# A two-block transformer kernel: last stage with row tiles stationary, inversion products in exchanged partition halves, boundaries started by one tile

## The reference

```
# first block, 272 rows: h = [meta; x]
h = h + rms_norm(diff_attention(rms_norm(h)), post0)
h = h + rms_norm(pool_mixer(rms_norm(h)), post1)
# second block, 256 rows
u   = rms_norm(h, pre_mix)
z   = u @ w_in                                  # splits into rwkv7, MLA and gates
mix = (g_rw * (rwkv7(z) @ w_b1) + g_mla * (mla(z) @ w_b2)) @ w_out
h   = h + rms_norm(mix, post_mix)
up  = causal_dwconv(rms_norm(h, pre_ffn) @ w_up)
h   = h + rms_norm((gelu(gate) * val) @ w_down, post_ffn)
e   = p @ w_ple                                 # p: 256 x 256
h   = h + rms_norm(sigmoid(h @ w_ple_gate) * e, ple_norm)
```

## Time and profile before

| | us |
|---|---|
| median of 3 executions | 2595.68 |
| lowest, highest | 2595.41, 2595.91 |
| profiled execution | 2592.1 |
| its span, first to last instruction | 2590.1 |
| mean granted TensorE clock | 0.993 of full speed |
| TensorE busy | 2508.2 |
| VectorE busy | 1634.2 |
| ScalarE busy | 1186.3 |
| GpSimd busy | 133.1 |
| bytes read from HBM | 418.14 MB at 163 GB/s over the span |

### The profile page before, as it was taken

How to read it: one execution, slowest core, us unless ns; L and a number is a source line. 1 busy time by engine, 2 the same in 40 slices (tenths; PEclk the granted TensorE clock), 3 DMA queues, 4 the chain that set the end, 5 groups by cost and what they waited for, 6 DMA issues and landing times.

```text
span 2590.1 us, 52387 instructions
## 1 busy us (share of the span) xinstructions
PE 2508.2 (97%) x22570; PEld 2458.2 (95%) x22570; DVE 1634.2 (63%) x1904; ACT 1186.3 (46%) x1630; POOL 133.1 (5%) x75
## 2 busy tenths in 40 slices
PE   8999999999999999999998999989999999999997
PEld 7999999989999889889897999989999999999997
DVE  6666676656555688487465545476666666666675
ACT  5444555544434562352345434455444444444563
POOL 0000000003500021031000000000000000000000
PEclk9999999999999999999999999999999999999999
DMA  6444444344555453242242465545545555555543
GB/s 226 158 151 162 144 149 161 130 147 164 180 193 180 158 210 116 77 169 87 97 162 98 169 225 181 194 151 181 193 178 188 185 180 192 178 187 185 180 178 114
DMA packets 60346, 424.58 MB, mean 164 GB/s; under 512 B 6544, under 2 KB 8720, under 8 KB 9648
## 3 DMA queue, kind: packets, MB, share of 16 engines
q1 hardware_dynamic: 60000, 421.72, 45.5%
q0 software_dynamic: 208, 0.77, 0.1%
HBM read 418.14 MB, written 4.33 MB: 163 GB/s over the span
## 4 chain that ended last, share of the span: by engine, by line
PE 87%; DVE 8%; ACT 2%; issue 1%; POOL 1%; DMA 0%; DVEq 0%; SPq 0%; POOLq 0%; ACTq 0%
PE banks L225 26%; PE banks L227 25%; PE banks L226 25%; DVE weights_lo_sb L200 2%; PE banks L279 1%; PE banks L281 1%; PE banks L280 1%; PE banks L1259 1%; PE banks L1272 1%; PE banks L607 1%; PE banks L1271 1%; PE banks L623 1%; POOL sums_sb L1021 0%; PE banks L1313 0%; PE banks L1703 0%
## 5 line engine op out<-in xcount | busy, mean ns | idle before, releaser
L225 PE MATMUL banks<-xa_hi_sb,weights_hi_sb 128*128 128x256 f32 (+1 forms) x4608 | 1315.9, 286 | 42.4 <-DVE xa_lo_sb L398 19.0
L227 PE MATMUL banks<-xa_hi_sb,weights_lo_sb 128*128 128x256 f32 (+1 forms) x4608 | 1302.6, 283 | 0.0
L226 PE MATMUL banks<-xa_lo_sb,weights_hi_sb 128*128 128x256 f32 (+1 forms) x4608 | 1300.6, 282 | 0.0
L200 DVE TENSOR_TENSOR weights_lo_sb<-raw_weights_sb,weights_hi_sb 128x1024 fp32r<-128x1024 f32 x786 | 939.9, 1240 | 271.2 <-ACT weights_hi_sb L186 265.3
L186 ACT CAST weights_hi_sb<-raw_weights_sb 128x1024 fp32r<-128x1024 f32 x786 | 780.1, 1049 | 573.1 <-DMA raw_weights_sb<-weights 572.8
L225 PEld LDWEIGHTS banks<-xa_hi_sb,weights_hi_sb 128*128 128x128 f32 x4608 | 870.3, 189 | 50.8 <-issue 39.1
L226 PEld LDWEIGHTS banks<-xa_lo_sb,weights_hi_sb 128*128 128x128 f32 x4608 | 873.1, 189 | 0.3
L227 PEld LDWEIGHTS banks<-xa_hi_sb,weights_lo_sb 128*128 128x128 f32 x4608 | 871.2, 189 | 0.0
L225 PE MATMUL banks<-xb_hi_sb,weights_hi_sb 128*128 128x256 f32 (+1 forms) x688 | 196.7, 286 | 4.8 <-DVE o_sb L866 2.0
L227 PE MATMUL banks<-xb_hi_sb,weights_lo_sb 128*128 128x256 f32 (+1 forms) x688 | 195.7, 284 | 0.0
L226 PE MATMUL banks<-xb_lo_sb,weights_hi_sb 128*128 128x256 f32 (+1 forms) x688 | 195.5, 284 | 0.0
(11 more groups left out here) (390 smaller groups left out, 2179.5 us busy)
## 6 DMA issues: line engine op xcount, KB each, us to landing
raw_weights_sb<-weights SPq DMA_DIRECT2D x393, 1024.0 KB, 4.8
h_sb<-h SPq DMA_DIRECT2D x4, 544.0 KB, 8.3
h_aside<-h_sb SPq DMA_DIRECT2D x1, 2176.0 KB, 11.3
h_sb<-h_aside SPq DMA_DIRECT2D x1, 2176.0 KB, 9.4
out<-h_sb SPq DMA_DIRECT2D x4, 512.0 KB, 2.9
masks_sb<-consts_rw POOLq DMA_DIRECT2D x1, 372.0 KB, 7.6
params_sb<-params SPq DMA_DIRECT2D x1, 305.5 KB, 5.2
consts_first_sb<-consts_first SPq DMA_DIRECT2D x1, 304.0 KB, 12.7
```

What stands on the lines that cost most here:

```text
L200: dve.tensor_tensor(c.w_lo[n % RAW][:, half], c.raw[n % RAW][:, half], c.w_hi[n % RAW][:, half].bitcast(F32), ALU.subtract).then_inc(c.sem ...
L225: pe.matmul(out, w_hi[:, k, a], x_hi[:, tile, cols], start=begin, stop=False)
L226: pe.matmul(out, w_hi[:, k, a], x_lo[:, tile, cols], start=False, stop=False)
L227: done = pe.matmul(out, w_lo[:, k, a], x_hi[:, tile, cols], start=False, stop=end)
```

## The change

Six edits:

1. **Boundaries.** VectorE scales, adds and lowers tile 0 alone, then tile 1, then goes on by pairs. ScalarE makes the high part of tile 0 on its own semaphore (`h_one`). TensorE starts the first slot with tile 0: eight products that want only its high part (L224, L225), then four with its low part (L228, waits `x_one`), then tile 1 on `x_ready`.
2. **Order of the first eight slots.** In `pool_in`, `ffn` and `ple_gate` the second slot is chunk 1's first (order 0, 4, 1, 2, 3, 5, 6, 7); it uses the same four tiles of x as the slot ahead of it. The sums `h_sums_pe` come ahead of slot 5, and VectorE's take of chunk 0 waits for one slot more.
3. **keep_busy.** Eight matmuls of constants (128x256, float32, into bank 1, nobody reads them) stand ahead of the first chunk at the first three boundaries.
4. **Square-root table.** A one-element square root is put ahead of chunk 3's squares in the outputs of attention, pool, mix and FFN, and after the last sigmoid; it loads the table there. The number of table loads stays 30.
5. **Inversion.** `lower_grams` runs a second time with the row halves swapped, 64 matmuls more per half of the heads, and `xx` is made from that in PSUM. `xx` and `tt` of a unit now lie in the partition half opposite to `yy`, so that in a level L1271's successor works from rows 1-q to columns 1-q and L1272's from rows 1-q to columns q, for q 0 and 1 in turn: the four use four different quarters of the array.
6. **The last stage by rows.** In `ple` and `ple_gate` a 128x128 tile of x (128 rows) is stationary and 512 columns of the weights move: 24 matmuls a slot instead of 48. Results have rows on partitions. ScalarE's Square with `accum_out` writes the row sums into a 128x1 column; sum, root and reciprocal are 128x1. The gain comes by two broadcast DMAs on GpSimd's queue and is multiplied in by VectorE. TensorE turns `h` by 32 transposes at the end (into all eight banks), and one `scalar_tensor_tensor` for each of 8 pieces of 128x512 computes y times root plus turned h; five stores, the last of 256 KB. The host no longer turns the result.

The core of the diff:

```diff
+        if single and half == 0:
+            (k, tile), pair = pair[0], pair[1:]
+            pe.wait_ge(c.sem("x_hi_ready"), KT * single + 1)
+            for j, out in outs:
+                a = slice(j * P, j * P + P)
+                pe.matmul(out, w_hi[:, k, a], x_hi[:, tile, cols], start=True, stop=False)
+                pe.matmul(out, w_lo[:, k, a], x_hi[:, tile, cols], start=False, stop=False)
+            pe.wait_ge(c.sem("x_one"), single)
+            for j, out in outs:
+                pe.matmul(out, w_hi[:, k, j * P:j * P + P], x_lo[:, tile, cols], start=False, stop=False)
...
-    scaled(0)
-    updated(0)
+            low_one(2 * q, None)
+            low_one(2 * q + 1, "x_ready")
+
+    st.did(scaled_one(0))
+    updated_one(0, "h_one")
+    scaled_one(1).then_inc(c.sem("y_scaled"), 1)
+    low_one(0, "x_one")
+    dve.wait_ge(c.sem("y_scaled"), done + 1)
+    updated_one(1, "h_ready")
+    scaled(1)
+    low_one(1, "x_ready")
+    updated(1)
...
+def keep_busy(c, pe, count, operand, bank):
+
+    for _ in range(count):
+        pe.matmul(c.ps[:, bank, 0:2 * P], operand[:, 0:P], operand[:, 0:2 * P], start=True, stop=True)
...
+FIRST_TWO = [0, 4, 1, 2, 3, 5, 6, 7]
+
+
+def first_two_pe(c, pe, n0, x, b, cols, squares):
+
+    keep_busy(c, pe, 8, c.consts, 1)
+    n = cols.stop - cols.start
+    for slot, m in enumerate(FIRST_TWO):
+        half, s = m // 4, m % 4
+        if m == 5:
+            h_sums_pe(c, pe, cols, squares)
+        products(c, pe, n0 + slot, x, [(k, 4 * s + k) for k in range(4)], banks(c, half, n), cols, s == 0, s == 3,
+                 ready=None if half else x_before(b) + 2 * s, single=b if m == 0 else None)
...
+    sqrt_table(c, act)
     act.wait_ge(c.sem("y_added"), Y_ADDED * (base // 4) + 2)
...
+        lower_grams(4, 0)
         kept_products(c, pe, 14)
         pe.wait_ge(S("grams_taken"), 3 * b + 1)
+        lower_grams(0, 1)
         grams(t["kt"], 2)
...
-                        m = pe.matmul(ps[at_[q], g, 64 * (u % 8):64 * (u % 8) + 64], t["lm"][at_[q], u, :],
+                        m = pe.matmul(ps[at_[1 - q], g, 64 * (u % 8):64 * (u % 8) + 64], t["lm"][at_[q], u, :],
...
-                            pe.matmul(ps[at_[q], 2 + g, cut], t["tt"][at_[q], u, :], t["xx"][at_[q], u, :], start=True, stop=True)
-                        m = pe.matmul(ps[at_[q], 4 + g, cut], t["xx"][at_[q], u, :], t["tt"][at_[q], u, :], start=True, stop=True)
+                            pe.matmul(ps[at_[1 - q], 2 + g, cut], t["tt"][at_[1 - q], u, :], t["xx"][at_[1 - q], u, :], start=True, stop=True)
+                        m = pe.matmul(ps[at_[q], 4 + g, cut], t["xx"][at_[1 - q], u, :], t["tt"][at_[1 - q], u, :], start=True, stop=True)
...
-        st.did(dve.tensor_tensor(t["xx"][:], t["ll"][:], mask("level0"), ALU.mult))
+        dve.wait_ge(S("grams"), 4 * b + 3)
+        swapped = ps[:, 0:2, :].rearrange("p b (u i) -> p (b u) i", u=8)
+        st.did(dve.tensor_tensor(t["xx"][:], swapped, mask("level0"), ALU.mult))
...
+        def tile_products(tile, ks):
+            for k in ks:
+                pe.matmul(out(tile), x_hi(k, tile), w_hi[:, k, :], start=s == k == 0, stop=False)
+                pe.matmul(out(tile), x_hi(k, tile), w_lo[:, k, :], start=False, stop=False)
+                m = pe.matmul(out(tile), x_lo(k, tile), w_hi[:, k, :], start=False, stop=s == k == 3)
+            return m
...
+    for tile in range(2):
+        for x in range(4):
+            pe.wait_ge(S("ple_gated"), 2 if tile == 0 else (3, 3, 4, 5)[x])
+            for k in range(4):
+                m = pe.transpose(c.ps[:, (2, 3, 0, 1, 4, 5, 6, 7)[4 * tile + x], P * k:P * k + P],
+                                 c.h[:, 4 * x + k, META + P * tile:META + P * tile + P], c.const("ident"))
+            m.then_inc(S("turned"), 1)
...
+    def gated(x, tiles):
+        act.activation(y[:, tiles, of_chunk(x)], c.ps[:, GATE_BANK[x] + tiles.start:GATE_BANK[x] + tiles.stop, :],
+                       ACT.Sigmoid).then_inc(S("ple_gated"), 1)
+
+    def squared(x, tile):
+        aside = (t["acc"], t["sq"], t["tmp"], t["ff"])[x][:].rearrange("p k r -> p (k r)")[:, of_chunk(tile)]
+        act.activation(aside, y[:, tile, of_chunk(x)], ACT.Square,
+                       accum_out=row_sums(c, x, tile)).then_inc(S("y_squared"), 1)
...
+    act.wait_ge(S("tile_done"), 3 * 4 + 1)
+    gated(3, slice(0, 1))
+    act.wait_ge(S("y_taken"), 20)
+    squared(3, 0)
+    act.wait_ge(S("slot_used"), n + 16)
+    gated(3, slice(1, 2))
+    sqrt_table(c, act)
+    rooted(0)
+    act.wait_ge(S("y_taken"), 21)
+    squared(3, 1)
+    rooted(1)
...
+    def rows_out(tile):
+        dve.wait_ge(S("root_done"), 9 + tile)
+        rs = c.small[:, 36 + tile:37 + tile]
+        st.did(dve.reciprocal(rs, c.small[:, 34 + tile:35 + tile]))
+        for x in range(4):
+            dve.wait_ge(S("turned"), HEADS + 4 * tile + x + 1)
+            bank = (2, 3, 0, 1, 4, 5, 6, 7)[4 * tile + x]
+            dve.scalar_tensor_tensor(out=y[:, tile, of_chunk(x)], in0=e[:, tile, of_chunk(x)], scalar=rs, in1=ps[:, bank, :],
+                                     op0=ALU.mult, op1=ALU.add).then_inc(S("h_ready"), 1)
...
+    for tile, a, z in ((0, 0, 2), (0, 2, 4), (1, 0, 2), (1, 2, 3), (1, 3, 4)):
+        cols = slice(SLOT_N * a, SLOT_N * z)
+        sp.wait_ge(c.sem("h_ready"), 4 * PAIRS + 4 * tile + z)
+        sp.dma_start(out[tile][:, cols], y[:, tile, cols]).then_inc(c.sem("out_written"), 16)
```

296 lines of the change are left out of this document (173 added, 123 removed).

## The result

| | kernel before | changed kernel |
|---|---|---|
| median | 2595.76 us (4 runs, 2595.41 to 2595.91) | 2559.22 us (4 runs, 2556.01 to 2562.92) |
| profiled execution | 2592.1 us | 2562.92 us |
| its span | 2590.1 us | 2561.0 us |
| granted clock | 0.993 | 0.995 |

The ratio is 0.986, 95% interval 0.9844 to 0.9876: faster, by 36.5 us between the medians, 29.2 us between the profiled executions. The forecast was 28.2 us, as 2563.9 for a profiled execution and 2567.5 for the median, range 2560 to 2581. Both facts need an explanation: that the sum came out nearly right was in good part luck, since its terms were wrong in both directions and two of the largest effects stood in none of them.

What follows compares the result with a forecast made beforehand. TensorE's work at its pace, its waits and the tail bound the kernel. Boundaries, inversion, last stage and tail sum to -28.2 us: profiled 2592.1 becomes 2563.9, plus 3.6 for the median 2567.5; range 2560 to 2581.

Steps and rivals of the forecast that it cites:

- its terms: Four boundaries -2.1, -0.7, -1.7, +0.35; inversion -12.4; last stage's pace -5.6; tail behind the last product -6.1 us.
- a slope: Last stage: pace at 256 and 272 columns, 0.41 ns a column, carried to 512: 222 ns a product, -5.6 us.

Runs made afterwards that it cites:

- pace_table: Bare products only, nothing of the kernel: moving operand's start address and column count varied; 115.3 to 121.7 ns at 256 columns, 229.3 at 512.
- pace_table2: Bare products only: stationary and moving start addresses both varied at 256 columns; 115.2 to 121.6 ns in the four-by-four table; 512 weight columns 234.9 to 236.6.
- xa64: Changed kernel, 160 unused bytes ahead of the FFN's operand tiles, second block's input at 256 columns a tile, 192 bytes later; median 2535.04 us, ratio 0.9809.

## What to carry to other kernels

When a table loses a column, every tile behind it moves, and a kernel bound by TensorE can change for that alone, here by 0.2% with 64 bytes and by 1% with both inputs placed: measure the pace by operand before crediting an edit, and place stationary and moving tiles deliberately, but check each stage and several executions, since the same places gave two paces. A pace of one size is no basis for a slope; measure the size in a kernel of bare products. And an edit in one place can move the clock's falls in another, so comparisons should be made at equal mean clock.

## What the runs showed of the hardware

- A float32r product of 256 columns takes 115.2 to 121.8 ns, mostly by the distance of the two operands' starts modulo 256 bytes (pace_table, pace_table2); in the kernel 113.3 to 120.0. At a distance of 192 bytes two paces occur, 115.3 to 115.7 and 119.6 bare, 113.3 and 117.8 in xa64.
- Below 256 columns it gains little: 112.3 ns at 128 columns, 112.9 at 192. Above: 125.2 or 127.1 at 272, 148.4 at 320, 229.3 to 236.6 at 512.
- The clock's falls differ between executions of one kernel with the same waits: 13.7 us at the scores in one profile of the changed kernel, 6.8 in the other; none there in the kernel before.
- 64x64 products that use the four quarters of the array in turn start every 14.8 ns, with two quarters every 29.7.
